# Hybrid decoder step with a gathered expert layer: projection passes regrouped, first tile selected in four groups, narrower level products

## The reference

```python
xn = rmsnorm(x, norm_mix_w)
proj = xn @ w_in                       # 1024 -> 2816, split into q, k, v, q_h, f_h, i_h, g_h
attn = softmax over a window of 128 with sinks and a bias by distance
o_h = gated recurrence over 4 heads of 128x128 state (q_h, f_h, i_h), normed, times silu(g_h)
h = x + concat(attn, o_h) @ w_o
hn = rmsnorm(h, norm_ffn_w)
# peer layer: 8 heads, each picks 16 of 128*128 experts
sc = hn @ w_q, against 2 x 128 sub keys of each head
sv, si = top_k(sc, 16); cand = sv[0][:, None] + sv[1][None, :]
fv, fi = top_k(cand, 16); eidx = the expert of fi; gate = softmax(fv)
act = gelu(u[eidx] . hn)               # a row of 1024 from u for each of 128 picks of a token
y = h + sum over picks of gate * act * v[eidx]   # and a row of 1024 from v
out = rmsnorm(y)
```

## Time and profile before

| | |
|---|---|
| median of 3 runs | 3190.39 us (3187.64 to 3194.28) |
| the profiled execution's own time | 3190.91 us |
| its span | 3188.8 us |
| PE, DVE, ACT, POOL busy | 81%, 75%, 48%, 65% |
| PE clock granted, mean | 0.971 |
| moved by DMA | 1214.05 MB, 381 GB/s over the span |

### The profile page before, as it was taken

How to read it: one execution, slowest core, us unless ns; L and a number is a source line. 1 busy time by engine, 2 the same in 40 slices (tenths; PEclk the granted TensorE clock), 3 DMA queues, 4 the chain that set the end, 5 groups by cost and what they waited for, 6 DMA issues and landing times. The chain is left out here.

```text
span 3188.8 us, 34779 instructions
## 1 busy us (share of the span) xinstructions
PE 2593.6 (81%) x8357; PEld 1380.7 (43%) x8357; DVE 2397.5 (75%) x5775; ACT 1524.5 (48%) x4133; POOL 2069.0 (65%) x2162
## 2 busy tenths in 40 slices
PE   7997899878977988688967887678767885778967
PEld 6853545445444544354434433343334432443321
DVE  2457777777887877887778878896888778776684
ACT  3415642366346643574346643573348433543333
POOL 1106575666766676667766777767776776676765
PEclk9999999999999999999998999999989999999989
DMA  8519999999999999999999999999999999999998
GB/s 289 196 46 350 361 409 381 412 404 410 400 403 395 410 409 409 388 410 409 407 382 390 401 409 409 394 392 409 409 399 386 405 408 409 367 408 410 409 393 341
DMA packets 360948, 1214.05 MB, mean 381 GB/s; under 512 B 43867, under 2 KB 70460, under 8 KB 359452
## 3 DMA queue, kind: packets, MB, share of 16 engines
q0 software_dynamic: 308288, 1121.46, 89.2%
q1 hardware_dynamic: 24588, 57.77, 4.8%
q10 hardware_dynamic: 27872, 32.61, 2.9%
HBM read 1191.24 MB, written 21.46 MB: 380 GB/s over the span
## 5 line engine op out<-in xcount | busy, mean ns | idle before, releaser
L1237 PE MATMUL ps<-rows,diag 128*128 128x256 f32 (+2 forms) x4224 | 1634.5, 518 | 515.8 <-DMA rows<-in_peer_v,idx 369.3
L1680 DVE CUSTOM_DVE_ANT_0 rows<-rows,ps 128x1024 f32<-128x1024 f32 x1056 | 1281.9, 1214 | 440.2 <-DMA rows<-in_peer_u,idx 437.6
L592 POOL DMA_INDIRECT rows<-in_peer_v,idx x1056 | 1022.3, 968 | 524.1 <-issue 241.0
L576 POOL DMA_INDIRECT rows<-in_peer_u,idx x1056 | 1021.6, 967 | 478.6 <-issue 245.9
L1237 PEld LDWEIGHTS ps<-rows,diag 128*128 128x128 f32 (+1 forms) x4224 | 752.4, 193 | 1269.2 <-issue 816.5
L869 ACT ACTIVATE act_g<-act_g 128x1 f32<-128x1 f32 x1056 | 211.9, 201 | 1196.1 <-DVE act_g L1680 1178.5
L1691 DVE SCALAR_TENSOR_TENSOR resid<-rows,act_g,resid 128x256 f32<-128x256 f32 x1024 | 493.4, 482 | 6.2 <-ACT diag L877 6.2
L877 ACT ACTIVATE diag<-ident,act_g 128x128 f32<-128x128 f32 x1024 | 411.3, 402 | 104.3 <-PE ps L1237 72.5
L873 ACT ACTIVATE act_g<-act_g,gate 128x1 f32<-128x1 f32 x1056 | 311.0, 294 | 34.3
L1116 PE MATMUL ps<-w_sc,r 128*128 128x512 f32 (+1 forms) x576 | 284.4, 593 | 0.9 <-DVE w_sc L1332 0.9
L987 PE MATMUL ps<-rows,bias 128*128 128x384 f32 (+1 forms) x608 | 211.2, 501 | 0.0
(11 more groups left out here) (291 smaller groups left out, 1886.3 us busy)
## 6 DMA issues: line engine op xcount, KB each, us to landing
bias<-in_w_in ACTq DMA_DIRECT2D x38, 512.0 KB, 6.8
rows<-in_peer_u,idx POOLq DMA_INDIRECT x1056, 9.4
rows<-in_peer_v,idx POOLq DMA_INDIRECT x1056, 9.4
r<-proj SPq DMA_DIRECT2D x7, 1344.0 KB, 8.8
w_sc<-in_w_q_t SPq DMA_DIRECT2D x8, 1024.0 KB, 8.5
proj<-staged ACTq DMA_DIRECT2D x41, 192.0 KB, 9.3
rows<-in_w_in POOLq DMA_DIRECT2D x14, 512.0 KB, 3.9
w_o<-in_w_in POOLq DMA_DIRECT2D x10, 512.0 KB, 6.3
```

Of the source, the lines that this page charges most:

```text
L576: nc.gpsimd.indirect_dma_start(ring[:, slot, :], None, a["peer_u"], bass.IndirectOffsetOnAxis(ap=idx[g % 2][:, k:k + 1], axis=0), engine_s ...
L592: nc.gpsimd.indirect_dma_start(ring[:, slot, :], None, a["peer_v"], bass.IndirectOffsetOnAxis(ap=idx[g % 2][:, k:k + 1], axis=0), engine_s ...
L1237: last = nc.tensor.matmul(Y[j][0:m, lo:512], diag[:, n % DIAGS, 0:m], ring[:, slot, 512 * j + lo:512 * (j + 1)], start=(k == 0), stop=(k = ...
L1680: V.tensor_tensor_reduce(ring[:, slot, :], ring[:, slot, :], hn_u, 1.0, 0.0, ALU.mult, ALU.add, col).then_inc(S["dots"], 1)
```

## The change

- **Passes.** Pass 2 takes tiles 2, 3 and the sample (288 columns), pass 3 tiles 4 to 7 (512 columns). Period -1 has no block; period 0 has all 22 of pass 2, periods 1 and 2 have 11 each of pass 3, period 3 none. A block of pass 3 is kept in two halves, the second two steps behind the first; both lie in one buffer and overlap in it, so that each waits for the landing of the store before. The bias is reloaded three times, not four.
- **Selection of tile 0** goes by four groups of two heads (`choose`), in `resid[1]`. Group 0 is chosen in period -1, right after its scores, and the gathers start on its 32 picks. The top lists of group 1 follow in period -1, the rest of group 1 and groups 2 and 3 stand between the steps 0 to 29 of period 0. The last four `fold_keys` and the last group of scores stand behind the scores of groups 0 to 2. `hn_u` is made before the selection.
- **Tile 1's projections** are loaded in two pieces, and its front has a table of its own, `TIMES_SECOND`; `TIMES_NEAR` holds for tiles 2 to 4.
- **Level products** multiply by the later halves alone, 64 columns, and `copy_predicated` takes 256 columns, not 512, except on the diagonal.
- **Sides.** In tile 0 DVE adds nothing for picks 0 to 47 and then all 512 columns of Y[0]; in tiles 1 and 2 384 columns, later 256 as before. PE does the rest of Y[0].
- **Ring.** Tile 0: u 7 slots, v 5. Tiles 1 and 2: u 6, v 5. From tile 3: u 8, v 7.

```diff
-U_SETS = {0: (0, 1, 2, 3, 12), 1: (8,), 4: (9, 10)}
-V_SETS = {0: (4, 5, 6, 7, 14, 13), 4: (11,)}
+U_SETS = {0: (0, 1, 2, 3, 12, 13, 8), 3 * PICKS: (8, 9)}
+V_SETS = {0: (4, 5, 14, 6, 7), 3 * PICKS: (10, 11)}
+U_LENT = {PICKS: (8,)}
-SIDE, SIDE_LAG = 2 * P, 3
+SIDE_LAG, SIDE_FROM = 3, 48
-PASS2 = 3 * P + NS
-PASS3 = 3 * P
+PASS2 = 2 * P + NS
+PASS3 = 4 * P
-BLOCK_AT = {-1: [96 + 2 * b for b in range(6)],
-            0: [28, 31, 34, 37, 77, 81, 84, 88, 91, 95, 98, 102, 106, 110, 114, 118],
-            1: [28, 32, 36, 78, 84, 90, 96, 102],
-            2: [8, 12, 16, 20, 74, 82, 90],
-            3: [8, 12, 16, 20, 74, 80, 86]}
-FOLD_AT = [40 + 2 * c for c in range(2 * PH)]
+BLOCK_AT = {0: [26, 29, 32, 35, 38, 41, 44, 47, 86, 88, 91, 93, 96, 98, 101, 103, 106, 108, 111, 113, 116, 118],
+            1: [28, 32, 36, 77, 83, 89, 95, 101, 107, 113, 119],
+            2: [28, 32, 36, 77, 82, 88, 93, 99, 104, 110, 115]}
+FOLD_AT = [40 + 2 * c for c in range(12)] + [90, 91, 92, 93]
...
+TIMES_FIRST |= {SCORE + c: 72 + 3 * c // 4 + 4 * (c // 24) for c in range(4 * DC)}
+TIMES_FIRST |= {TOP + x: t for x, t in enumerate((79, 80, 96, 97, 133, 136, 146, 149))}
+TIMES_FIRST |= {G_CAND + g: t for g, t in enumerate((81, 128, 140, 151))}
+TIMES_FIRST |= {G_PICK + g: t for g, t in enumerate((82, 130, 142, 154))}
+TIMES_FIRST |= {G_GATED + g: t for g, t in enumerate((98, 132, 145, 157))}
...
+    return (4 * P if k >= SIDE_FROM else 0) if g == 0 else 3 * P if g < 3 else 2 * P
...
+            def keep_later(b, part):
...
+                if part == 0:
+                    act.wait_ge(S["block"], b + 1)
+                    if b + 2 not in PARTS and b + 1 not in PARTS:
+                        act.dma_start(wp_later[j], a["w_in"][(b + 2) % CHUNKS]).then_inc(S[f"w_b{j}"], 16)
+                if b or part:
+                    act.wait_ge(S["proj_out"], stores_before(b) + 16 * part)
+                out = staged[:, P * part:P * part + 2 * P]
...
                     if block_at(p, k - 1) is not None:
-                        keep_later(p, block_at(p, k - 1))
+                        keep_later(block_at(p, k - 1), 0)
+                    if p and block_at(p, k - 3) is not None:
+                        keep_later(block_at(p, k - 3), 1)
...
-                                lhs = rhs = lev[l % 2].rearrange("p (c t) -> p c t", c=4)
+                                lhs = lev[l % 2].rearrange("p (c t) -> p c t", c=HG)
+                                rhs = later_halves(lhs, LEVELS[l])
+                                out = F[l % 2][:, 0:HG * P // 2].rearrange("p (c x m) -> p c x m", c=HG, m=LEVELS[l])
...
             for g in range(TILES + 1):
-                pool.wait_ge(S["idx_done"], g + 1)
+                if g:
+                    pool.wait_ge(S["idx_done"], chosen(g))
...
+                    if g == 0 and k < PICKS and k % GPICKS == 0:
+                        pool.wait_ge(S["idx_done"], k // GPICKS + 1)
```

More of the change, by code:

```diff
@@ L264, in build @@
         diag = sb("diag", [P, DIAGS, P])
[L265 removed]
+        staged = sb("staged", [P, STAGE])
         ident = sb("ident", [P, P])
@@ L571, in gather_u @@
                 slot, earlier, use = U_SLOTS[PICKS * g + k]
-                if use == 1 and slot in (12, 13):
-                    pool.wait_ge(S["block"], len(BLOCK_AT[-1]))
                 if earlier is not None:
@@ new lines, in keep_later @@
+                if b < CHUNKS:
+                    nc.scalar.activation(staged_s, bank[:, 2 * P:PASS2], ACT.Copy)
+                last = nc.scalar.activation(out, bank[:, pair], ACT.Copy)
+                if b < CHUNKS or part:
+                    last.then_inc(S["kept_b"], 1)
+                    act.wait_ge(S["kept_b"], b + 1)
+                else:
+                    own.mark(last)
+                    own.settle()
+                first = 2 if b < CHUNKS else 4 + 2 * part
+                act.dma_start(proj[first:first + 2, :, place(c), :].rearrange("i p t -> p i t"),
+                              out.rearrange("p (i t) -> p i t", t=P)).then_inc(S["proj_out"], 16)
@@ L995, in turn, with spread_norm @@
                 return last
+            def spread_norm(g, f):
+                if g is None:
+                    pe.wait_ge(S["kept"], CHUNKS)
+                    pe.wait_ge(S["consts_in"], 16 * 10)
+                else:
+                    pe.wait_ge(S["dots"], PICKS * (g + 1))
+                for c in range(DC):
+                    last = nc.tensor.matmul(hn_u[:, P * c:P * (c + 1)], w_ffn_t[:, c:c + 1].to_broadcast([P, P]), ident[:, :],
+                                            start=True, stop=True)
+                last.then_inc(S["w_spread"], 1)
             def front(k, f):
@@ L1018, in front @@
                         last.then_inc(S["g_turned"], 1)
-                    if k == 4 and not first:
+                    if k == 4 and f == 1:
+                        pe.wait_ge(S["proj_in"], 32)
+                        pe.wait_ge(S["sc_kept"], 4)
+                        nc.tensor.transpose(F[2][:, 0:P], slots(C_V, 1)[:, 0, :], ident[:, :]).then_inc(S["turned"], 1)
+                    if k == H_TURN:
+                        pe.wait_ge(S["rest_in"], 16)
+                        pe.wait_ge(S["p_kept"], 2 * f + 2)
+                        for c in range(4):
+                            nc.tensor.transpose(F[0][:, P * c:P * (c + 1)], slots(C_I + c, 1)[:, 0, :], ident[:, :])
+                        for c in range(4):
+                            last = nc.tensor.transpose(F[1][:, P * c:P * (c + 1)], slots(C_G + c, 1)[:, 0, :], ident[:, :])
+                        last.then_inc(S["i_turned"], 1)
+                    if k == 4 and f >= 2:
                         pe.wait_ge(S["proj_in"], 32 * f)
@@ L1266, in _ @@
                 for k in [*steps(p), *range(PICKS, PICKS + SUM_LAG)]:
-                    if f is not None and k == (PICKS if f else BLOCK_AT[-1][0]):
+                    if f and k == PICKS:
                         spread_norm(g, f)
```

329 lines of the change are left out of this document (213 added, 116 removed).

## The result

The change made the kernel slower: 3203.6 us in the median of 9 runs (3193.9 to 3211.8) against 3190.1 for the kernel before (9 runs, 3187.2 to 3195.1), a ratio of 1.0044 with a 95% interval of 1.0032 to 1.0056. In a later group of runs it stood at 1.0065 (1.0041 to 1.0088). The forecast was 3173, with 3146 to 3200 as its range, so it was wrong in sign too. The profiled execution has a span of 3204.8 us, against 3188.8, and the DMA engines moved the same 1214.05 MB in both.

What follows compares the result with a forecast made beforehand. Steps were taken as bound by DMA bytes, with about 100 us before them waiting for tile 0's selection. Terms -31 - 2 + 6 - 3 + 8 + 10 + 10 - 16 = -18 on 3190.9 gave 3173 us, range 3146 to 3200.

Steps and rivals of the forecast that it cites:

- Step 1: Before tile 0's first dot: choosing two heads first starts dot 0 at about 222 instead of 253.1, -31 us.
- Step 2: Steps 0 to 28 of tile 0: sides leave DVE, the remaining selection enters, DVE bounds at 80 us, -2 us.
- Step 3: Steps 28 to 48 of tile 0: wider rows and more blocks load PE, 70 us in all, +6 us.
- Step 4: Steps 48 to 86 of tile 0: three blocks gone, PE and DVE under the bytes' pace, 99 us, -3 us.
- Step 5: Step 86 to tile 1's first dot: 13 blocks for 9, 5 us of bytes plus 3 for DVE, +8 us.
- store chain: Rival, steps 86 to 118: copies wait for store landings, intervals 11.2 us, +38, 3211 us; 0.17 with v ring's upper end.
- Step 6: Periods 1, 2 and 3: more blocks in the first two, none in the third: +10, +10 and -16 us.
- The v ring: Periods 1 and 2: one v slot less adds 1.7 and 1.2 us, between bounds of 0 and 127 us.
- The halves of pass-3 blocks: Periods 1 and 2: second halves wait for stores likewise, two steps (5.3 us) after the first; no cost in the sum.
- The bytes of period 1: Period 1: 11 blocks for 8 and 0.5 MB more of `xn_3`, 3.4 MB, +8.3 us.
- Step 7: Level products on 64 columns: PE gains nothing, DVE at most 1 us of the start, counted as 0.
- The named threshold: Periods 1 and 2: a DMA share under 0.98 there would make the forecast wrong.

Runs made afterwards that it cites:

- f1: Changed kernel with slot 13 back in v, second half of pass-3 blocks one step later, slot 9 as second stage for odd pass-2 blocks: 3167.8 us.
- d3: Changed kernel with slot 13 out of the rings until tile 3, used as two stages, one store a block: 22.5 us faster than d2.
- d2: Changed kernel with slot 13 in no ring until tile 3 (u 6, then 5; v 5): 3207.1 us.
- d1: Changed kernel with slot 13 given back from u to v, so v has 6 slots up to tile 3: 15.6 us less than d2.
- e3: Changed kernel with slot 13 in v and the second half of a pass-3 block three steps after the first, not two: 3178.8 us, ratio 0.9975.
- f3: Kernel before with only the level products on 64 columns: 3189.3 against 3190.1 us, ratio 0.9997.

## Why the prediction was wrong

**Step 1, the start (-31): right.** Measured -33.9. Scores began at 181.07 (182.7 forecast), `idx` for 32 picks was ready at 203.2, the gather at 204.08 (205.3), dot 0 at 219.2 (222).

**Step 2 (-2): right.** -1.9, with DVE busy 74.05 of 79.7 us (77 of 80 forecast).

**Step 3 (+6): right in kind.** 73.0 and 69.4 us in two profiles, against 70. PE was busy for 69.55 us in the first, above the 67 forecast, but at a clock of 0.95; at 1.00 it was 65.98 in the second. With a second stage the stretch takes 66.3 to 67.0, so some 2 to 5 us of it were the wait for stores, which the step had not counted at all.

**Step 4 (-3): right,** -1.8.

**Step 5 (+8): too small,** by its trace: +13.4. The step counts 13 blocks where 14 are kept, and +2.1 MB, 5 us; the stretch moved 3.3 MB more (52.42 to 55.69), which at 410 GB/s is 8 us. f1 moves as much as the changed kernel, at 408 GB/s where before had 394, and has +4.2. What f1 took away, 9 us, is part store chain and part v slot: the second stage alone takes 10 (d3 against d2), the v slot alone 5 to 6 (d1), and the two cover each other. The store chain came at a third of the rival's price: intervals of 8.9 us, where the sum took 8.0 and the rival 11.2. It named the right line and the right wait. The wait ended 8.5 and 8.4 us after the issue of the store to `proj_s` in the two copies shown, where the median was 9.6. The prediction held against the rival that such a store is smaller and lands sooner when ACT holds the ring back; no run tells these two apart.

**Step 6 (+10, +10, -16): the step that failed.** The changed kernel had +21.9 and +24.2 in periods 1 and 2, and -15.1 in period 3. Three terms were wrong:

- The v ring, "+1.7 and +1.2" between bounds of 0 and 127. The slot is worth 12 to 21 us in the whole of the changed kernel, and 15 up to tile 3 in the kernel before. The argument was that 63.0 us of waits for side sums stood beside a DMA share of 1.02 and so cost nothing, and that one step later would be hidden by the same backlog. With 5 slots the same kind of wait costs, so its being free with 6 said nothing of the next slot. A share of 1.02 says that the queue isn't empty, not that it has one gather to spare.
- The halves of pass-3 blocks. The rival's text says that they "wait in the same way", but the sum of step 6 gives them nothing. That rival's price was worked out for steps 86 to 118 alone; the 22 blocks of periods 1 and 2, each with two waits, were the larger place for it. The stage took 8 us off each period (d3 against d2), the later half 7 and 11 (e3 against d1).
- The bytes of period 1, "3.4 MB, +8.3". The blocks did bring 2.9 MB more, but period 1 moved no more bytes in all (148.99 and 148.55 MB). Before, two reloads of the bias stood in it, issued from 641 and 935 us; in the changed kernel one, from 627. The reload that is gone left period 1, and the sum took it out of period 3. The gathers' queue moved 2.7 MB less besides. Period 2 had 4.4 MB more for 3.6.

So the number of period 3 was luck in part. Its bytes fell by 3.3 MB (143.87 to 140.60), not 6.1, which is 8 us; the other 7 of the 15.1 are its rate, 408 GB/s for 400.

With the ring and the wait mended a rest is left. At the bytes of the changed kernel e3 has +8.5 and +12.9, f1 +7.4 and +13.6, and f1's second trace +10.9 and +15.6 in periods 1 and 2, at 395 to 398 GB/s. In period 1 this can't be bytes. What still keeps the rate under 405 there, no run shows.

**Step 7 (0): right.** A level of 64 columns took 1.00 to 1.10 us, one of 128 columns 1.06, and f3 shows no difference. The table in the Trainium skill, TensorE: Matmul & The Clock Gate, Back-to-back issue gap, is for a product by itself and would have these at half the time; the same section says that in a stream of weight loads and products both set the spacing. The trace agrees with the latter: 8 records take 1.00 to 1.10 us at 64 columns and 1.06 at 128.

The sum missed by 34 us on the profiled execution (+16.0 against -18): 26.1 in periods 1 and 2, 5.4 in step 5, 3.2 in step 3, 1.2 in step 4, less 2.9 of the start and with some 1 us in what follows. The named threshold, "a DMA share under 0.98 over periods 1 and 2", was not reached at 0.99 and 1.00, though the forecast was wrong: the share fell by 2 to 3 hundredths while the rate fell from 405 to 381 GB/s. The rate was the better witness. With the costs mended (e3: 3178.8, f1: 3167.8) the kernel is where the sum had put it, 3173; since the bytes of periods 1 and 3 were not as summed, part of that is luck. So is the nearness of the store chain's 3211 to the 3204 and 3213 measured: it had +38 in steps 86 to 118, where the sum missed 5.4.

## What to carry to other kernels

Where two streams take turns in one in-order queue, a buffer more for one is worth nothing while the other waits at the head: read each stream's waits for its own slots, and move a slot only to the stream that waits. A wait that costs nothing beside a saturated DMA may have no margin left, so price the loss of a buffer by an experiment or by its upper bound, not by today's stall. When an in-order engine's side job ends in a wait for a landing, give that wait a price at every place where it will stand, and look first for room that is free just then (here slot 9 in tile 0) and for another place in the queue.
